# A hybrid state-space and attention trunk: real and imaginary halves exchanged by transfers, low-rank input in two passes

## The reference, cut to what matters

```python
def s5_mixer(u, lam_re, lam_im, log_dt, b_re, b_im, c_re, c_im, d_skip, w_glu, b_glu):
    ...
    lam_bar = jnp.exp(lam * dt)
    b_bar = ((lam_bar - 1.0) / lam)[..., None] * b_c
    bu = jnp.einsum('blgi,gpi->blgp', uf.astype(jnp.complex64), b_bar)
    a = jnp.broadcast_to(lam_bar, bu.shape)
    _, states = lax.associative_scan(_s5_combine, (a, bu), axis=1)
    y = jnp.real(jnp.einsum('blgp,gip->blgi', states, c_c))
    y = y + d_skip.astype(jnp.float32).reshape(S5_GROUPS, S5_GROUP) * uf
    g = jax.nn.gelu(y)
...
def gla_mixer(q, k, v, a_lr, w_a2, b_a, norm_w):
    ...
    log_a = jax.nn.log_sigmoid(a_lr.astype(f32) @ w_a2.astype(f32) + b_a.astype(f32)) / GLA_TAU
```

## Time and profile before

| | us |
|---|---|
| median of three runs | 1936.49 (1932.54 to 1936.99) |
| the profiled execution | 1935.79 |
| its span, first to last instruction | 1934.0 |
| TensorE busy | 1742.5 (90%) |
| VectorE, ScalarE, GpSimd busy | 848.5, 575.1, 401.3 |
| mean granted TensorE clock | 0.961 of full |

### The profile page before, as it was taken

One profiled execution on the slowest core, in us unless ns is written; L12 is line 12 of the kernel. 1 busy time (PEld: TensorE's weight loads), 2 busy tenths in 40 slices (PEclk: granted clock), 3 DMA queues, 4 the chain that ended last, 5 costly groups with the idle time before them and its releaser, 6 DMA issues. The chain is left out here.

```text
span 1934.0 us, 23734 instructions
## 1 busy us (share of the span) xinstructions
PE 1742.5 (90%) x7974; PEld 1397.9 (72%) x7974; DVE 848.5 (44%) x1628; ACT 575.1 (30%) x1491; POOL 401.3 (21%) x519
## 2 busy tenths in 40 slices
PE   1997898899999854897979999999999999989998
PEld 1875676777777643686866688888888888867886
DVE  3868533356565444333322423433333444344443
ACT  3622211155545431223322502222222233122211
POOL 1866000000000022675840001222222122000000
PEclk9998998999999977898989999999999999999999
DMA  7445554445454298554631333333333333265653
GB/s 182 127 128 168 149 152 124 128 137 150 138 156 142 70 274 301 180 174 137 179 93 50 125 98 112 112 107 120 106 118 101 112 101 99 82 204 148 195 182 109
DMA packets 325154, 269.40 MB, mean 139 GB/s; under 512 B 84840, under 2 KB 264872, under 8 KB 325048
## 3 DMA queue, kind: packets, MB, share of 16 engines
q1 hardware_dynamic: 308568, 257.49, 43.8%
q10 hardware_dynamic: 16480, 10.56, 1.8%
HBM read 161.49 MB, written 106.49 MB: 139 GB/s over the span
## 5 line engine op out<-in xcount | busy, mean ns | idle before, releaser
L2116 PE MATMUL odd_acc<-ht_hi,odd_w_hi 128*128 128x512 f32 x800 | 333.0, 416 | 9.8 <-DVE odd_w_lo L1958 9.8
L2116 PE MATMUL odd_acc<-ht_lo,odd_w_hi 128*128 128x512 f32 x800 | 314.4, 393 | 0.0
L2116 PE MATMUL odd_acc<-ht_hi,odd_w_lo 128*128 128x512 f32 x800 | 312.9, 391 | 0.0
L1063 PE MATMUL ev_acc<-ht_hi,ev_w_hi 128*128 128x512 f32 x576 | 244.9, 425 | 1.4 <-DVE ht_lo L785 1.4
L1063 PE MATMUL ev_acc<-ht_lo,ev_w_hi 128*128 128x512 f32 x576 | 227.9, 396 | 0.0
L1063 PE MATMUL ev_acc<-ht_hi,ev_w_lo 128*128 128x512 f32 x576 | 227.4, 395 | 0.0
L2116 PEld LDWEIGHTS odd_acc<-ht_hi,odd_w_hi 128*128 128x128 f32 x800 | 150.8, 189 | 51.0 <-DVE odd_w_lo L1958 10.0
L2116 PEld LDWEIGHTS odd_acc<-ht_lo,odd_w_hi 128*128 128x128 f32 x800 | 150.4, 188 | 33.4
L2116 PEld LDWEIGHTS odd_acc<-ht_hi,odd_w_lo 128*128 128x128 f32 x800 | 151.0, 189 | 29.8
L1970 DVE TENSOR_TENSOR odd_stage<-odd_acc,rms_rows 128x512 f32<-128x512 f32 x96 | 66.4, 692 | 227.4 <-PE odd_acc L2116 227.4
L1567 PE MATMUL out_acc<-wo_hi,mix_hi 128*128 128x512 f32 x256 | 107.2, 419 | 47.2 <-POOL mix_lo L1459 41.7
(11 more groups left out here) (296 smaller groups left out, 3158.5 us busy)
## 6 DMA issues: line engine op xcount, KB each, us to landing
odd_gl_in<-scr_heads SPq DMA_DIRECT2D x32, 640.0 KB, 4.3
mix_raw<-scr_mix SPq DMA_DIRECT2D x32, 512.0 KB, 4.1
scr_heads<-odd_stage SPq DMA_DIRECT2D x64, 256.0 KB, 2.0
odd_w_raw<-od_w_in SPq DMA_DIRECT2D x48, 256.0 KB, 3.5
ev_s_tables<-scr_s_tables SPq DMA_DIRECT2D x32, 320.0 KB
ev_w_raw<-ev_w_in SPq DMA_DIRECT2D x36, 256.0 KB, 4.5
ev_x_tile<-x SPq DMA_DIRECT2D x16, 512.0 KB, 3.8
ev_s_cos_sin<-scr_s_cos_sin SPq DMA_DIRECT2D x32, 256.0 KB
```

Of the source, the lines that this page charges most:

```text
L1063: mm = pe.matmul(acc[n % 3][:], w[j][:, k, :], h[:, k, t], start=(k == 0 and r == 0), stop=(k == KT - 1 and r == 2))
L2116: mm = pe.matmul(acc[n % 4][:], w[j][:, k, :], h[:, k, t], start=(k == 0 and q == 0), stop=(k == KT - 1 and q == 2))
```

## The change

In the state space, the two products with exchanged halves go. `inputs` makes one product; ScalarE copies it out (`take_v`, new); two transfers per group exchange its halves within SBUF (`swap_v`, new, 64 partitions of 1 KB each way); VectorE's `scan`, one slot later than before, multiplies by cosine, by sine and sign, adds, and scans; two more transfers exchange the halves of the scanned states (`swap_z`, new); `turn_back` (new), another slot later, combines them into a `pz` of half the size; `outputs` makes two products. With that the tables `bmq` and `cq`, their VectorE and ScalarE operations and their stores go, and a group's table is 384 columns instead of 640. In the odd layer, group 0 makes two passes instead of three: the low part of its weights stands in columns 32 to 47 of the high tile, so rows 32 to 47 of the product carry it; `w2` is loaded twice, at rows 0 and 32 of a tile set to zero, and `gate` sums both.

```diff
                 def load_stream(i):
...
+                def swap_halves(dst, src, sem):
+                    for h in range(2):
+                        sp.dma_start(dst[h * ST:(h + 1) * ST], src[(1 - h) * ST:(2 - h) * ST]).then_inc(sem, 16)
+
+                def swap_v(i):
+                    sp.wait_ge(v_out, i + 1)
+                    swap_halves(v_sw, v, v_swapped)
+
+                def swap_z(i):
+                    sp.wait_ge(z_ready, i + 1)
+                    swap_halves(z_sw, z, z_swapped)
...
+                    i = stream_at(p, S_IN(0) + 1)
+                    if i is not None:
+                        swap_z(i)
+                    i = stream_at(p, S_IN(0))
+                    if i is not None:
+                        swap_v(i)
...
                     a.copy(bm[:], ps_bt).then_inc(bm_ready, 1)
-                    a.copy(bmq[:, :, 0:ST], ps_bt[:, :, ST:P]).then_inc(bm_ready, 1)
-                    a.mul(bmq[:, :, ST:P], ps_bt[:, :, 0:ST], -1.0).then_inc(bm_ready, 1)
...
+                def take_v(i):
+                    act.wait_ge(v_done, i + 1)
+                    if i:
+                        act.wait_ge(z_ready, i)
+                    a.copy(v[:], ps_vin).then_inc(v_out, 1)
...
-                    for out, n0, first, second, op in ((cp, 0, 0, 1, ALU.add), (cq, 1, 1, 0, ALU.subtract)):
...
+                    ch.mark(d.tensor_tensor(cp[:], pw(pw_r), yy(0), ALU.mult))
+                    tt(bpt[:], pw(pw_i), yy(1), ALU.mult)
+                    d.tensor_tensor(cp[:], cp[:], bpt[:], ALU.add).then_inc(cp_ready, 1)
...
                 def scan(i):
                     j = i % 2
-                    dve.wait_ge(v_done, i + 1)
-                    ch.link(d.tensor_tensor(v[:], ps_vw, cs[:, j], ALU.mult))
-                    dve.sem_inc(v_used, 1)
-                    tt(v[:, 0], v[:, 0], v[:, 1], ALU.add)
-                    ch.link(d.tensor_tensor_scan(z[:], r8[:, i:i + 1].broadcast_to([P, NC]), v[:, 0], 0.0, ALU.mult, ALU.add))
+                    cos, sin = cs[:, j, 0], cs[:, j, 1]
+                    dve.wait_ge(v_swapped, 32 * (i + 1))
+                    if i == 0:
+                        dve.wait_ge(made, 6)
+                    ch.mark(d.tensor_tensor(v_rot[:], v[:], cos, ALU.mult))
+                    ch.link(d.scalar_tensor_tensor(v_sw[:], v_sw[:], sgn, sin, ALU.mult, ALU.mult))
+                    tt(v_rot[:], v_rot[:], v_sw[:], ALU.add)
+                    d.tensor_tensor_scan(z[:], r8[:, i:i + 1].broadcast_to([P, NC]), v_rot[:], 0.0, ALU.mult,
+                                         ALU.add).then_inc(z_ready, 1)
+
+                def turn_back(i):
+                    j = i % 2
+                    cos, sin = cs[:, j, 0], cs[:, j, 1]
+                    dve.wait_ge(z_swapped, 32 * (i + 1))
                     if i:
                         dve.wait_ge(y_done, i)
-                    d.tensor_tensor(pz[:, :, 1:], z[:].unsqueeze(1).broadcast_to([P, 2, NC]), cs[:, j],
-                                    ALU.mult).then_inc(pz_ready, 1)
+                    ch.mark(d.tensor_tensor(pz[:, 1:], z[:], cos, ALU.mult))
+                    ch.link(d.scalar_tensor_tensor(z_sw[:], z_sw[:], neg, sin, ALU.mult, ALU.mult))
+                    d.tensor_tensor(pz[:, 1:], pz[:, 1:], z_sw[:], ALU.add).then_inc(pz_ready, 1)
...
-                    i = stream_at(p, S_IN(0))
+                    i = stream_at(p, S_IN(0) + 2)
+                    if i is not None:
+                        turn_back(i)
+                    i = stream_at(p, S_IN(0) + 1)
...
+                    sp.wait_ge(made, 5)
+                    for at_ in (0, LO_AT):
+                        sp.dma_start(w2[at_:at_ + RANK], prm["gla_w_a2"][0].rearrange("r (h d) -> r h d", h=GH)).then_inc(prm_in, 16)
...
+                    passes = ((w_hi, ht_hi), (w_hi, ht_lo)) if g == 0 else ((w_hi, ht_hi), (w_lo, ht_hi), (w_hi, ht_lo))
```

More of the change, by code:

```diff
@@ L201, in even_layer @@
         r8 = sb("s5_r8", [P, 48])
-        halfs = sb("eps_half", [P, 2])
-        eps, half = halfs[:, 0:1], halfs[:, 1:2]
+        halfs = sb("eps_half", [P, 4])
+        eps, half, sgn, neg = (halfs[:, k:k + 1] for k in range(4))
         K1 = 1024
@@ L214, in even_layer @@
         A = 8
[L215 to L222, removed]
+        tab = at("s5_tables", A, [P, 2, 3 * P])
+        cs = at("s5_cos_sin", A + 3, [P, 2, 2, NC])
+        ut = at("s5_u", A + 7, [P, 2, NC])
+        v, v_sw, v_rot = (at(n, A + 9 + k, [P, NC]) for k, n in enumerate(("s5_v", "s5_v_swapped", "s5_v_turned")))
+        z, z_sw = at("s5_z", A + 12, [P, NC]), at("s5_z_swapped", A + 13, [P, NC])
+        pz = at("s5_pz", A + 14, [P, NC + 1])
+        e = at("s5_gelu", A + 15.25, [P, NC])
+        go = at("s5_out", A + 16.25, [P, 2, NC])
         xt = at("x_tile", A, [P, XB, D])
@@ L295, in even_layer @@
         ld, zero_made = c.sems("s5_ld", 2), c.sem("s5_zero_made")
[L296 to L297 removed]
+        (v_done, v_out, v_swapped, z_ready, z_swapped, pz_ready, y_done, squared, arg_ready, tanh_done, g_ready) = (c.sem("s5_" + n) for n in (
+            "v_done", "v_out", "v_swapped", "z_ready", "z_swapped", "pz_ready", "y_done", "squared", "arg_ready", "tanh_done", "g_ready"))
         g_st = c.sems("s5_g_st", 2)
@@ L500, in _ @@
                 pool.wait_ge(made, 2)
+                g.memset(sgn[0:ST], 1.0).then_inc(made, 1)
+                g.memset(sgn[ST:P], -1.0).then_inc(made, 1)
+                pool.wait_ge(made, 4)
+                g.memset(neg[0:ST], -1.0).then_inc(made, 1)
+                g.memset(neg[ST:P], 1.0).then_inc(made, 1)
+                pool.wait_ge(made, 6)
                 ch = Chain(pool, pchain)
@@ L1610, in odd_layer @@
     N_GATE = GH * NB
+    LO_AT = 32
     def columns(g):
@@ L1655, in odd_layer @@
         ot = at("gl_out", 30, [P, 2, 2, GB])
-        low, w2 = at("ga_low", 0, [RANK, SEQ]), at("ga_w2", 8, [RANK, GH, DK])
+        low, w2 = at("ga_low", 0, [LO_AT + RANK, SEQ]), at("ga_w2", 8, [LO_AT + RANK, GH, DK])
         gm, ge = at("ga_min", 11, [P, 2, BLK]), at("ga_exp", 15, [P, 2, BLK])
@@ L2039, in _ @@
                 dve.wait_ge(made, 4)
-                dve.wait_ge(prm_in, 64)
+                v.memset(w2[:], 0.0).then_inc(made, 1)
+                dve.wait_ge(prm_in, 80)
                 split(0)
@@ L2113, in products @@
                     j = g % 2
+                    passes = ((w_hi, ht_hi), (w_hi, ht_lo)) if g == 0 else ((w_hi, ht_hi), (w_lo, ht_hi), (w_hi, ht_lo))
                     for k in range(k0, k0 + KT // 2):
-                        for q, (w, h) in enumerate(((w_hi, ht_hi), (w_lo, ht_hi), (w_hi, ht_lo))):
+                        for q, (w, h) in enumerate(passes):
                             mm = pe.matmul(acc[n % 4][:], w[j][:, k, :], h[:, k, t], start=(k == 0 and q == 0),
-                                           stop=(k == KT - 1 and q == 2))
+                                           stop=(k == KT - 1 and q == len(passes) - 1))
                     return mm
```

69 lines of the change are left out of this document (34 added, 35 removed).

## The result

| | before | after |
|---|---|---|
| median (us) | 1934.99 (1932.54 to 1936.99, 4 runs) | 2126.66 (2121.97 to 2128.2, 4 runs) |
| ratio, 95% interval | | 1.0987 [1.0964, 1.1011] |
| span of the profiled execution | 1934.0 | 2126.4 |
| mean granted TensorE clock | 0.961 | 0.918 |

Slower, as forecast, but by 192 us instead of 67, and above the range that ended at 2085. To see where it went, the span is cut at three events that both kernels have: the first `inputs`, `outputs(13)` (the last one before attention), and `outputs(31)` (the last one). Each is the start of a TensorE row in the timeline.

A forecast was written before the change was run, and what follows sets the result against it. TensorE was taken as the bound (1742.5 of 1934.0 us). Build -13, loop before attention +45, beside attention +41 and low rank -6.4 gave +66.6; 1935.8 + 66.6 + 0.7 = 2003 us, range 1920 to 2085, holding 0.80.

The forecast's parts named there:

- the landing of v's exchange: State-space group chain: v's two transfers within SBUF land in 2.1 us, plus 0.4 for the second issue: 2.5 us.
- A calm group: State-space loop, undisturbed part: the new chain sums to 12.0 us, 12.8 with slow restart, against 10.37 before.
- `outputs` to SyncE's release: Start of the group chain: two products until SyncE is released, 1.06 us; output products slower after idling, 0.43 more each.
- long waits: Loop before attention: two groups meeting late loads delay `scan`, z's transfers and `turn_back`, +8 us each, +16 together.
- The rival of 2093 us: State-space loop: exchanges stay behind bulk transfers, landing in 4.5 us instead of 2.1; calm groups over 16 us; chance 0.17.
- receipts heaviest in HBM: Exchanges within SBUF: by this skill rule landings would be near 1.4 us, the sum some 22 us smaller, 1981.
- The build: State-space tables: less VectorE work shortens TensorE's wait for `powers_of_c`, none of ScalarE's wait counted: -13 us.
- Products taken away: State-space loop: two of five products per group go, up to -28 us, only where TensorE sets the pace.
- Beside attention: Eighteen groups: VectorE's order adds +0.3 or +1.8 us in turn (+19), traffic and restarts +22: +41 us.
- traffic and slow restarts: Loop beside attention: `load_qkv` and weight loads ahead of swaps, with slow TensorE restarts, +1.2 us a group, +22.
- Before attention: State-space loop: six calm groups +15, five beside the build +14, two meeting late transfers +16: +45 us.
- Low rank: Odd layer, group 0: one of three passes goes, -7.2 us; later start of `split(0)` costs +0.8: -6.4 us.

The follow-up runs named there:

- with the load spread: Changed kernel with the cosine load as two transfers of 64 partitions each instead of one that reads 64 rows twice: 1999.91 us, ratio to before 1.0348.
- the load cut by columns: Kernel before with the cosine load cut between cosines and sines, each half still repeating its source twice: 1939.33 us, ratio 1.0025.
- the two splits: Changed kernel with the cosine load as two transfers: of 64 partitions each, 1999.91 us; cut between cosines and sines, each source still repeated twice, 2134.97 us.
- the kernel where nobody waits: Changed kernel with cosine load in two 64-partition transfers; exchanges go to a spare tile, VectorE takes unexchanged halves without waiting: 1903.56 us, ratio 0.9836.
- the kernel before with the load spread: Kernel before with only the cosine load split into two transfers of 64 partitions: 1909.86 us, ratio 0.988.

## Why the prediction was wrong

**The failed step is the landing of v's exchange.** The sum took 2.1 us and 0.4 for the second issue, from rows of transfers that wait behind no narrow one; in after v takes 8.33 us, because two of the sixteen DMA engines are held by the cosine load ahead. A calm group, step by step (with the load spread, the shortest of the six):

| step (us) | forecast | after | load spread |
|---|---|---|---|
| `outputs` to SyncE's release | 1.06 + 0.8 | 2.10 | 1.16 |
| loads and store issued | 2.25 | 2.31 | 2.89 |
| v exchanged | 2.5 | 8.33 | 2.92 |
| `scan` | 2.0 | 2.03 | 2.03 |
| z exchanged | 2.5 | 2.56 | 2.61 |
| `turn_back`, hand-overs | 1.3 + 0.4 | 1.34 | 1.33 |
| group | 12.8 | 18.67 | 12.94 |

In after every step but one is within 0.4 us. The one is off by 5.8 in a calm group; over all 32 groups, spreading the load took off 127 / 32 = 4.0 us each. For z the price of 2.1 was right.

That the total with the load spread, 1999.9, is close to the forecast of 2003 is in good part luck. Spreading the load also takes 25 us from the kernel before. Laid against that kernel, the change costs 1999.9 - 1909.9 = 90 us, where +66.6 was forecast, of which +16 was for long waits that are then gone. By stretch it is -12.2, +58.8, +52.4 and -9.1. So the sum was too small in other terms too. A calm group is 14.5 us in the mean and not 12.8: with the loads and the store it takes 2.9 to 3.7 us and not 2.25, and v 2.9 to 3.8 and not 2.5.

**The rival of 2093 us** had the right place, but bulk as the cause, and the wrong size. It put 4.5 us on both exchanges, for bulk ahead of them; z's median landing stayed at 2.0 and v cost 8.3 in a calm group, and 2.9 to 3.8 behind the same bytes once these were spread. What was right in it is that increments wait behind an earlier transfer, on the engines that both use. And the row that spoke for it, the 256 KB store `scr_q` with 6.7 us against 2.0, owes more than half of the difference to the narrow load as well: in the kernel before its median is 4.1 us with the load spread, and 6.5 with the load cut by columns. Its condition was that calm groups pass 16 us, and 18.67 did.

By the Trainium skill (DMA: Bandwidth & Descriptors, Rules for kernel authors), a leading zero-stride broadcast of c copies "confines the whole DMA to at most c engines". The trace agrees, with a share of 0.12 to 0.15 where two of sixteen are 0.125 and four late increments of 32, and so do the two splits, 1999.9 against 2135.0 us. The prediction weighed the section on completion order, and not this rule, which named the load in plain words. The other rule that it weighed, receipts heaviest in HBM (its section is on transfers that GpSimd issues; these are SyncE's), would have put exchanges within SBUF near 1.4 us; z's landed at 2.0, like 256 KB to HBM in the earlier trace rows. No gain from the target's place is seen.

**The build, -13 forecast, -13.2 measured.** TensorE over 110 us to the first `inputs`, before and after (busy times of PE, PEld, DVE, ACT, POOL, then the granted clock), and its waits there in after:

```profile
110.00:216.00 106.00, 83.93 (x362) 62.50 (x360) 79.69 (x133) 24.93 (x61) 49.34 (x37) 0.92 0.52 158
```

```profile
110.00:203.00 93.00, 80.93 (x365) 60.32 (x363) 66.10 (x97) 20.44 (x38) 47.48 (x37) 0.98 0.48 146
```

```profile
PE ev_bank L1131 <- DVE ev_s_cpow L929: 5.2, 3, 3.0
PE ev_bank L1131 <- ACT ev_s_kernel L693: 4.2, 1, 4.2
PE ev_bank L1123 <- DVE ev_s_bpow L914: 2.6, 3, 1.5
```

The wait for `powers_of_c` went from 14.3 us in this stretch to 5.2, that for `copy_ker` from 7.7 to 4.2, and 2.6 came new for `powers_of_b`: -10.0. The other -3.0 are TensorE's busy time for the same products, at a granted clock of 0.98 instead of 0.92. The sum was right with other parts: ScalarE's wait was given nothing and gave 3.5, the clock was not counted, the new wait neither.

**Products taken away.** Where the chain doesn't bind, a calm group is 9.51 us: that term is shown. It was right to give none of it to the sum.

**Beside attention, +41 forecast, +112.4 measured,** +52.3 with the load spread. The order on VectorE was read rightly for the groups of 14.39 us: 14.7 was forecast, and 14.7 is what most of them take when no transfer is waited for. The rest, 300.2 - 252.9 = 47 us, comes with the waits for the two exchanges, where +1.8 for nine groups and +22 for traffic and slow restarts were taken. Part of it is idle time and part TensorE's clock. The granted clock between 450 and 600 us was 0.82 in after, 0.91 with the load spread, and 1.00 in before and in the kernel where nobody waits:

```profile
450.00:600.00 150.00, 112.39 (x444) 84.14 (x445) 63.77 (x165) 52.14 (x192) 0.00 (x0) 0.82 0.37 108
```

From `outputs(13)` to `outputs(31)` TensorE was busy 273 us in after, 253 with the load spread and 235 where nobody waits, for the same 1103 matmul records. So of the +112.4 about 38 are the clock, and the sum had at most 18 x 0.86 = 15.5 for that, within its +22. Of the 47 us some 18 are the clock.

**Before attention, +45 forecast, +94.5 measured,** and +36.8 with the load spread; against the kernel before with the load spread it is the +58.8 above.

**Low rank, -6.4 forecast.** Alone it gave -8.4 us (1935.27 to 1926.83). In its profile group 0 takes 16.33 us instead of 23.23, -6.9 where the passes were put at -7.2. The +0.8 was wrong: the wait at the layer's start did not grow but fell, from 9.85 to 9.1 us, and to 8.6 in after. The two loads of `ga_w2` took SyncE 2.14 us in after, against 1.86 for one in the earlier trace rows, so the second did not add up to 1.86:

```profile
1210.63 2.14 SPq L1803 DMA_DIRECT2D odd_ga_w<-gla_w_a  x2
...
1213.83 0.58 SPq L1806 DMA_DIRECT2D odd_causal<-causal  x1
```

Behind the first `gate` it is 1.0 us longer, which the sum did not have. Together that is -6.6: the forecast of -6.4 held, and the other 2 us of the -8.4 cannot be put down to the edit, as the next stretch shows. In after the rest is only 1.5 us shorter, because from `outputs(31)` to the first product of the output projection it took 142.9 us, against 137.2 in before. No edit touches that stretch, and it took 137.7 with the load spread and 134.3 with the low rank alone: a profile can't tell less than some us there.

## What to carry to other kernels

Before a small transfer is put on the critical path, look at the share of DMA engines in windows of one us behind what is issued ahead of it: a tail at 2/16 is the sign of a transfer that uses two engines, and a transfer over all sixteen that is issued behind it, in that queue or another, waits for those two. A load that repeats its source with a small outer dimension is such a transfer, and cutting it into transfers whose outer dimension is the partitions is worth trying even where nobody seems to wait for it. And add up the chain by its hand-overs, each with its own row: that told each step but the wrong one to 0.4 us in after. It is still a lower bound: with the wrong price put right, the best calm group met it to 0.2 us and the mean of six was 1.7 above.

## What the hardware showed that was not expected

- A load of 256 KB with a source repeated twice held the DMA engines at a share of 0.09 to 0.15 and 31 to 53 GB/s for some five us; an exchange of 2 x 64 KB issued 1.9 us later was usable 8.33 us after its issue, against 2.92 with the same bytes spread.
- Another engine's queue is little shelter from it: 6.92 us from issue to use, against 3.6 to 4.5 from the same queue with the load spread.
- The increments of a semaphore tell how many DMA engines are late: 28 of 32 came within 2.8 us of the issue in the group shown, the last four after 8.0 to 8.3.
- The narrow load already cost the kernel before 25 us (1934.4 to 1909.9), 16.8 of them in waits that the profile puts down to the load of the inputs (`ev_s_u`), the last issued of the three that are waited for together.
